# The first expert stage loads whole 2 MiB weight units into five homes, in place of 1 MiB halves into eleven

## The reference

```
logits = (xt @ w_router) + b_router
top_v, top_i = lax.top_k(logits, TOP_K);  gates = softmax(top_v)
y = sum over e of dense_gate[:, e] * ((silu(xt @ w1[e]) * (xt @ w3[e])) @ w2[e])
```

## Time and profile before

| what | value |
|---|---|
| median of 3 runs | 1507.8 us (1507.69 to 1508.5) |
| profiled execution | 1507.31 us |
| its span, first to last instruction | 1505.5 us |
| PE busy | 1423.2 us, 95% |
| DVE busy | 841.7 us, 56% |
| ACT busy | 566.9 us, 38% |
| bytes moved, mean rate | 443.45 MB, 295 GB/s |
| granted TensorE clock, mean | 0.99 |

### The profile page before, as it was taken

One profiled execution on the slowest core, in us unless ns is written; L12 is line 12 of the kernel. 1 busy time (PEld: TensorE's weight loads), 2 busy tenths in 40 slices (PEclk: granted clock), 3 DMA queues, 4 the chain that ended last, 5 costly groups with the idle time before them and its releaser, 6 DMA issues.

```text
span 1505.5 us, 24226 instructions
## 1 busy us (share of the span) xinstructions
PE 1423.2 (95%) x10246; PEld 1001.3 (67%) x10246; DVE 841.7 (56%) x1358; ACT 566.9 (38%) x838; POOL 32.7 (2%) x32
## 2 busy tenths in 40 slices
PE   6999999999999999999899988999999999999987
PEld 6988879999988888873588437984443443443435
DVE  5777697899979679940589107772211212112127
ACT  5673337464443447730477003432111111110115
POOL 0000101000030000000000001000000000000001
PEclk9999999999999999999999999999999999999999
DMA  9441026454441239999999994599999999999991
GB/s 355 163 168 59 2 95 228 176 213 179 168 155 60 84 126 418 408 365 409 406 419 370 420 420 167 203 427 378 426 427 425 427 427 427 427 426 427 425 420 56
DMA packets 48354, 443.45 MB, mean 295 GB/s; under 512 B 6768, under 2 KB 7280, under 8 KB 17008
## 3 DMA queue, kind: packets, MB, share of 16 engines
q1 hardware_dynamic: 47088, 438.36, 71.7%
q10 hardware_dynamic: 1152, 3.46, 0.6%
HBM read 440.75 MB, written 1.05 MB: 293 GB/s over the span
## 4 chain that ended last, share of the span: by engine, by line
PE 74%; DVE 12%; DMA 8%; ACT 3%; issue 2%; PEldq 0%; DVEq 0%; ACTq 0%; PEld 0%; SPq 0%
PE psum L239 72%; DMA sb_spare<-moe_up 3%; DMA sb_work<-moe_up 3%; DVE sb_ring_r L1280 2%; DMA sb_ring<-moe_last 1%; DMA sb_work<-moe_last 1%; DVE sb_work L3040 1%; PE psum L2825 1%; DVE sb_ring_r L298 0%; PE psum L2230 0%; DVE sb_work L1374 0%; DVE sb_ring_r L524 0%; DVE sb_ring_r L2152 0%; DVE sb_work L1800 0%; DVE sb_work L1372 0%
## 5 line engine op out<-in xcount | busy, mean ns | idle before, releaser
L239 PE MATMUL psum<-sb_work 128*64 128x512 f32 (+13 forms) x3548 | 323.6, 342 | 23.5 <-DVE sb_work L3040 7.8
L239 PEld LDWEIGHTS psum<-sb_work 128*64 128x64 f32 (+5 forms) x3548 | 161.7, 143 | 160.7 <-issue 139.1
L239 PE MATMUL psum<-sb_ring,sb_work 128*64 128x512 f32 (+2 forms) x660 | 159.0, 599 | 12.7 <-DMA sb_ring<-moe_last 5.2
L239 PE MATMUL psum<-sb_xT_r,sb_ring_r 128*128 128x256 f32 x512 | 143.9, 283 | 0.0
L239 PE MATMUL psum<-sb_split 128*128 128x512 f32 (+1 forms) x398 | 128.7, 382 | 0.0
L239 PEld LDWEIGHTS psum<-sb_ring,sb_work 128*64 128x64 f32 (+1 forms) x660 | 51.5, 141 | 104.2 <-issue 98.1
L3038 DVE TENSOR_TENSOR sb_work<-sb_work,psum 128x512 f32<-128x512 f32 x16 | 11.0, 688 | 167.9 <-ACT sb_work L2950 167.9
L2950 ACT ACTIVATE sb_work<-psum 128x512 f32<-128x512 f32 x16 | 9.6, 598 | 240.2 <-PE psum L239 240.2
L239 PEld LDWEIGHTS psum<-sb_xT_r,sb_ring_r 128*128 128x128 f32 x512 | 98.2, 192 | 0.3
L3008 DVE SCALAR_TENSOR_TENSOR sb_out_even<-psum,sb_work,sb_out_even 128x512 fp32r<-128x512 f32 x32 | 22.6, 747 | 125.8 <-ACT sb_out_even L2936 125.8
L239 PE MATMUL psum<-sb_split,sb_lnp_r 128*128 128x512 f32 (+1 forms) x260 | 87.7, 376 | 4.1 <-DVE sb_ring_r L2152 3.7
(11 more groups left out here) (514 smaller groups left out, 2876.6 us busy)
## 6 DMA issues: line engine op xcount, KB each, us to landing
sb_work<-moe_up SPq DMA_DIRECT2D x33, 2048.0 KB, 25.8
sb_ring<-moe_wide SPq DMA_DIRECT2D x52, 1024.0 KB, 9.6
sb_ring<-w_dense SPq DMA_DIRECT2D x23, 2048.0 KB, 8.7
sb_work<-moe_wide SPq DMA_DIRECT2D x43, 1024.0 KB, 10.6
sb_ring<-moe_up SPq DMA_DIRECT2D x18, 2048.0 KB, 25.3
sb_work<-moe_down SPq DMA_DIRECT2D x17, 2048.0 KB, 24.0
sb_ring<-ffn_wide SPq DMA_DIRECT2D x14, 2048.0 KB, 7.5
sb_ring<-moe_down SPq DMA_DIRECT2D x9, 2048.0 KB, 25.2
```

The source lines that it names most:

```text
L239: return nc.tensor.matmul(o, lhsT, rhs, start=start, stop=stop, **kw)
```

## The change

Loads are made per unit and no longer per half. `M1_LOADS` has one entry per unit and expert (72 in place of 144); there are five homes of 4096 columns: the three ring slots and two in `work`. The eleventh home is given up. A home may be refilled when half b of the unit in it was used. The first unit comes in three pieces (a quarter, a quarter and a half of it), so its half a is waited for on a semaphore of its own. The readers still go by halves, but both halves of a unit land together.

```diff
-        M1_HOMES = (2, 3, 4, 5, 0, 1, 6, 7, 8, 9, 10)
-        LAST_DOWN = 2 * M1_STREAM.index("d2")
+        M1_HOMES = (1, 2, 0, 3, 4)
         M1_LOADS = []
         for m in range(len(MEMBERS)):
-            own_loads = [(m, i, j) for i in range(NH) for j in range(len(MEMBERS[m])) if not (m > 0 and packed(m - 1) and i < 2)]
+            own_loads = [(m, s, j) for s in range(len(M1_STREAM)) for j in range(len(MEMBERS[m]))
+                         if not (m > 0 and packed(m - 1) and s == 0)]
             if packed(m) and m < LAST_MEMBER:
-                own_loads[-PACK * (NH - LAST_DOWN):-PACK * (NH - LAST_DOWN)] = [(m + 1, 0, 0), (m + 1, 1, 0)]
+                own_loads[-PACK:-PACK] = [(m + 1, 0, 0)]
             M1_LOADS += own_loads
...
         def half_raw(m, i, j=0):
-            return home_columns(ring, work[:, SPLIT_AT + HOMES_AT:], emb.rearrange("p h d -> p (h d)"), M1_LOAD_AT[m, i, j], half_size(i))
+            return home_columns(ring, work[:, SPLIT_AT + HOMES_AT:], M1_LOAD_AT[m, i // 2, j], half_first(i), half_size(i))
...
         def half_loaded(eng, m, i, j=0):
-            n = M1_LOAD_AT[m, i, j]
-            eng.wait_ge(home_sem(n), 16 * (n // len(M1_HOMES) + 1) + (32 if n % len(M1_HOMES) == HOMES2 else 0))
+            if (m, i) == (0, 0):
+                eng.wait_ge(sem("first_loaded"), 48)
+                return
+            n = M1_LOAD_AT[m, i // 2, j]
+            eng.wait_ge(home_sem(n), 16 * (n // len(M1_HOMES) + 1))
...
         def m1_load_used(eng, n):
-            m, i, _ = M1_LOADS[n]
-            eng.wait_ge(sem("m1_pe"), M1_PE[m, M1_HALVES[i]])
+            m, s, _ = M1_LOADS[n]
+            eng.wait_ge(sem("m1_pe"), M1_PE[m, M1_STREAM[s] + "b"])
...
-                    to = half_raw(m, i, j)
+                    to, first = unit_raw(n), 0
                     if n == 0:
                         sp.dma_start(to[:, 0:QUARTER], src[:, 0:QUARTER]).then_inc(sem("piece_loaded0"), 16)
-                        to, words = to[:, QUARTER:], slice(QUARTER, HALF)
-                    sp.dma_start(to, src[:, words]).then_inc(home_sem(n), 16)
+                        sp.dma_start(to[:, QUARTER:HALF], src[:, QUARTER:HALF]).then_inc(sem("first_loaded"), 16)
+                        first = HALF
+                    sp.dma_start(to[:, first:], src[:, first:unit_size(unit)]).then_inc(home_sem(n), 16)
```

More of the change, by code:

```diff
@@ L2078, in m1_home, with home_columns, unit_size, unit_raw @@
             return M1_HOMES[(n + HOME_SHIFT) % len(M1_HOMES)]
-        def home_columns(ring_tile, rest, last, n, size):
+        def home_columns(ring_tile, rest, n, first, size):
             h = m1_home(n)
[L2083 to L2087, removed]
+            if h < RING:
+                return ring_tile[:, h, first:first + size]
+            at = UNIT * (h - RING) + first
             return rest[:, at:at + size]
+        def unit_size(s):
+            return half_size(2 * s) + half_size(2 * s + 1)
+        def unit_raw(n):
+            return home_columns(ring, work[:, SPLIT_AT + HOMES_AT:], n, 0, unit_size(M1_LOADS[n][1]))
         def half_raw(m, i, j=0):
-            return home_columns(ring, work[:, SPLIT_AT + HOMES_AT:], emb.rearrange("p h d -> p (h d)"), M1_LOAD_AT[m, i, j], half_size(i))
+            return home_columns(ring, work[:, SPLIT_AT + HOMES_AT:], M1_LOAD_AT[m, i // 2, j], half_first(i), half_size(i))
         def half_low(m, i):
-            return home_columns(ring_r, split[:, HOMES_AT:], m1_emb, M1_LOAD_AT[m, i, 0], half_size(i))
+            return home_columns(ring_r, split[:, HOMES_AT:], M1_LOAD_AT[m, i // 2, 0], half_first(i), half_size(i))
         def home_sem(n):
-            r = n % len(M1_HOMES)
-            return sem("first_loaded" if r == HOMES2 else f"home_loaded{r}")
+            return sem(f"home_loaded{n % len(M1_HOMES)}")
         def half_loaded(eng, m, i, j=0):
-            n = M1_LOAD_AT[m, i, j]
-            eng.wait_ge(home_sem(n), 16 * (n // len(M1_HOMES) + 1) + (32 if n % len(M1_HOMES) == HOMES2 else 0))
+            if (m, i) == (0, 0):
[3 more added lines that the diff above has]
+            eng.wait_ge(home_sem(n), 16 * (n // len(M1_HOMES) + 1))
         def half_number(m, i):
@@ L2116, in m1_load_used @@
         def m1_load_used(eng, n):
-            m, i, _ = M1_LOADS[n]
-            eng.wait_ge(sem("m1_pe"), M1_PE[m, M1_HALVES[i]])
+            m, s, _ = M1_LOADS[n]
+            eng.wait_ge(sem("m1_pe"), M1_PE[m, M1_STREAM[s] + "b"])
         def m1_home_loads(r):
-            return len(range(r, len(M1_LOADS), len(M1_HOMES)))
+            return len(range(r, len(M1_LOADS), len(M1_HOMES))) if r < len(M1_HOMES) else 0
         def m1_last_loads(s):
-            return [n for n in range(len(M1_LOADS) - len(M1_HOMES), len(M1_LOADS)) if m1_home(n) // 2 == s]
+            return [n for n in range(len(M1_LOADS) - len(M1_HOMES), len(M1_LOADS)) if m1_home(n) == s]
         def split_high(act, m, i):
@@ L3691, in _ @@
                 expert_at = {}
-                for n, (m, i, j) in enumerate(M1_LOADS):
+                for n, (m, unit, j) in enumerate(M1_LOADS):
                     position = MEMBERS[m][j]
@@ L3697, in _ @@
                         m1_load_used(sp, n - len(M1_HOMES))
-                    s, words = M1_STREAM[i // 2], slice(half_first(i), half_first(i) + half_size(i))
+                    s = M1_STREAM[unit]
                     src = I["moe1_wide"][expert_at[position], WIDE.index(s)] if s in WIDE else I["moe1_last"][expert_at[position], NARROW.index(s)]
-                    to = half_raw(m, i, j)
+                    to, first = unit_raw(n), 0
                     if n == 0:
                         sp.dma_start(to[:, 0:QUARTER], src[:, 0:QUARTER]).then_inc(sem("piece_loaded0"), 16)
-                        to, words = to[:, QUARTER:], slice(QUARTER, HALF)
-                    sp.dma_start(to, src[:, words]).then_inc(home_sem(n), 16)
+                        sp.dma_start(to[:, QUARTER:HALF], src[:, QUARTER:HALF]).then_inc(sem("first_loaded"), 16)
+                        first = HALF
+                    sp.dma_start(to[:, first:], src[:, first:unit_size(unit)]).then_inc(home_sem(n), 16)
                 overflow_sync(sp, 0)
```

## The result

The changed kernel takes 1522.0 us (median of 4 runs, 1519.3 to 1528.4) against 1508.0; the ratio is 1.0098, 95% interval 1.0074 to 1.0121, that is **+14.8 us** (+11 to +18); the two medians differ by 14.0. Forecast were 1512.8 us, +5.0. The direction was right, the size a third of it, and 1522.0 lies outside the forecast range of 1507.0 to 1517.5. The profiled execution took 1519.3 us (span 1517.5), the fastest of the four. Its first expert load is issued at 549.75 us and not at 551.28, so times of the stage are compared as distances from this issue.

The account below looks back on a forecast made before the run. It took the expert stage to end with the DMA stream, set back by homes freed late: member 3 begins 3.0 us later, d2 of member 5 5.0 later in all, so 1507.8 + 5.0 = 1512.8 us, range 1507.0 to 1517.5.

Parts of the forecast that it names:

- The mechanism of member 2: Member 2: u1' must wait for all of u0, not only u0a; 3.4 us of depth lost, landing 7.5 us after issue.
- The start: First expert loads: u0a lands only with u0b, delaying the first splits; cost 0.3 us, bounds 0 and 2.5.
- u1 of member 3: Member 3's tight load: ready at 759.5, PE comes at 760.7; covered by about 1 us, else PE loses 0 to 1.
- Behind u1' the queue stays fed: pairs are released 2 or more loads ahead: Member 2: the 5 wide and 6 narrow units left take 46.6 us, so d2' lands at 735.6, d2 4.0 us later.
- u1' waits for u0 ... landing at 863.7: Member 5: u0 used at 856.2, u1' lands 7.5 us later; 41.7 us of loads follow, the last landing at 905.4.
- the queue's bound: Member 2: queued behind g1' and u1, u1' would land at 687.9; issue at 681.5 plus 7.5 decides, 1.1 us later.
- The clock: Packed members: low level after PE's waits; member 2 called even, member 3 begins +2.0 or +4.0 (taken +3.0), member 5's d2 +4.3 to +6.2.
- Rate beats depth: Rival: lost depth is hidden in the expert stage and faster transfers take all 6.2 us off, 1501.6 us; chance 0.10.
- No change: Rival: PE's waits spread out, never reaching the low clock, lone loads near the queue's bound; +1.1, 1508.9 us; chance 0.22.
- The much slower rival: Rival: the start loses 2.5 us, u1 of member 3 1 us, low clock in both packed members 2.2; +10.7, 1518.5; chance 0.08.
- signs named for being right: Deeper rate dips, lone units 7 to 9 us, PE's waits from d0, d2 near 735.6 (member 2) and 906 (member 5).
- signs named for being wrong: Member 2's d2 at or before 731.6, PE waiting on splits in members 0, 1, 3, 4, or granted clock at 1.00 throughout.

Follow-up runs that it names:

- experiment 5: The change with dummy matmuls on PE ahead of its waits for loads in members 2 and 5, half as many as in an earlier try: +11.5 us, ratio 1.0076.
- late rows: The change with ACT's load of the norm's rows (1 MiB) issued only after the last expert load landed, not at the start of member 5: +11.2 us, ratio 1.0074.
- experiment 3: The change with each unit loaded in two transfers of a half, readers waiting for both halves, homes freed by unit: +15.8 us, ratio 1.0105.

## Why the prediction was wrong

**What held.** The bytes and the place did: all is lost in the packed members, behind u0. The mechanism of member 2 came out to the tenth. u1' was issued when u0 was used and took 7.5 us; the loads issued then, and the one that waited for member 3's g0, in the kernel after:

```profile
679.62 0.85 SPq L3710 DMA_DIRECT2D sb_work<-moe_wide  x2
...
749.94 0.33 SPq L3710 DMA_DIRECT2D sb_ring<-moe_wide  x1
```

and the time to landing of u1' of member 2 (issued at 679.62) and of member 5 (858.55):

```profile
sb_work<-moe_wide SPq DMA_DIRECT2D x1, 2048.0 KB, 7.5
```

```profile
sb_work<-moe_wide SPq DMA_DIRECT2D x1, 2048.0 KB, 10.2
```

A full queue's units landed 4.90 us apart and narrow ones 3.70 (4.91 and 3.68 were taken). The start cost nothing in place of 0.3: members 0 and 1 are done at 111.8 in both. Members 3 and 4 took 96.3 us in both, so u1 of member 3 was covered.

**The step that failed** is the sentence "Behind u1' the queue stays fed: pairs are released 2 or more loads ahead", and with it the 46.6 us of the loads behind u1'. From the landing of u1' (687.2) to that of d2' (736.9, PE starts at 737.04) it took 49.8 us, 3.2 more. The loss has two parts, of about the same size.

The first comes directly behind u1', before PE has waited for more than 0.41 us. d0 was issued 0.5 us behind u1', but landed 6.46 us after it and not 4.91:

```profile
sb_work<-moe_wide SPq DMA_DIRECT2D x1, 2048.0 KB, 13.5
```

So a queue that had almost run dry (u1, the last load in it, landed 1.4 us after u1' was issued) delayed two loads: the first landed 7.5 us after its issue, as I had priced it, the second 13.5 us after its own, where 7.5 + 4.91 - 0.5 = 11.9 had been priced. d0' made up 0.15 us of it, so that 1.4 us of the 3.2 are lost here.

The second part is the one I had left out of the working: I had worked out when PE would wait, for d2, but not carried a wait back into the releases that follow it. PE waits 4.12 us for d0' and gets the low clock; d0 is used at 707.3, and only then are the loads of u2' and d1 issued (707.47 and 707.98), when the queue has one load left, to land at 709.5. u2', d1 and d1' then land 4.34, 6.07 and 4.75 us apart, 1.7 us more than a full queue's. The rate falls with PE at work all the time, in this window after:

```profile
707.00:714.00 7.00, 7.00 (x60) 4.04 (x58) 0.00 (x0) 0.92 (x3) 0.00 (x0) 1.00 0.82 312
```

From the issue of u1' to the landing of d2' the forecast had 7.5 + 46.6 = 54.1 us; it took 57.3, and 56.1 with dummies in place of the waits (experiment 5). So the clock behind the waits makes 1.2 us of the 3.2.

**Member 5** had the same mistake at another place. "u1' waits for u0 ... landing at 863.7" took 7.5 us for a lone load, and I didn't ask for the queue's bound. It took 10.2, because the queue was behind already: g1, three loads ahead of it, landed at 853.40, and three loads at 4.90 us make 868.1, where u1' landed at 868.7. The bound as I had worked it out in member 2, from an idle queue at the issue of g1' (847.7 + 7.5 + 2 x 4.9 = 865.0), would have missed it too. That is 2.7 us; from there to the last landing it was 41.8 us against 41.7. Whether the norm's 1 MiB was part of it is open: late rows left it at 9.5.

**The clock** was mis-sized. I called member 2 even and took the middle; the low level came in d0 and in d2 of member 2 and in d1 of member 5, where PE began d2 2.6 us behind the last landing (913.11, 910.5) in place of 1.0.

**The sum by terms**, as distances from the first issue. d2 of member 2 begins 7.0 us later (forecast 4.0): 3.2 more by the queue, 0.3 less by the start, 0.1 of rest. Member 3 begins 6.8 later (forecast 3.0): those 3.0 again and 0.8 of the clock, since d2 took 7.07 us, near the 7.2 of before, where the forecast had the middle between that and 5.2. In member 5 the forecast added 2.2 and the trace 6.6: 2.7 by u1', 1.6 because PE began d2 2.6 us behind the last landing and not 1.0 (d1 had waited 4.42 us and run at the low level), 0.1 of rest. That makes 13.4 in the traces; the 14.8 of all runs has 1.4 more, which one pair of traces doesn't show. The forecast's own middle is a little off: that of 3.3 to 7.2 is 5.2 or 5.3, and I wrote 5.0.

**The rivals.** "Rate beats depth" is refuted by its own sign: d2 of member 2 begins 7.0 us later and not sooner. With equal homes and equal waits, 71 more transfers cost 1.0 us (experiment 3), and 6.2 lies just outside what the two intervals leave room for. The full queue is faster by 0.09 us per unit (2.097 MB at 419 and at 427 GB/s), but where the queue is full the time isn't set. "No change" (1508.9) is out by the interval. The much slower rival (1518.5) was the nearest in size, by the wrong reason: neither the start nor u1 of member 3 took part. What neither it nor my forecast had is the size of depth: the forecast priced 3.4 us of later issue for 1 MiB less and unit grain together, and the runs give 5.9 and 7.7 us for each alone.

**The signs.** Of the signs named for being right, the dips are deeper (by 8 and 20 GB/s over 32 us), a lone unit took 7.5 us, though the other 10.2, and PE's waits begin ahead of d0, even with 0.41 us at u1. The two starting times of d2 came out too late: 7.0 us later in member 2, where 4.0 was forecast, and 13.4 in member 5, where 5.2 was. None of the signs named for being wrong appeared.

## What to carry to other kernels

Where a queue of prefetches feeds an engine that alternates between being slower and faster than the loads, count the depth in bytes that can be in flight while a home is still held, not in homes: a home twice as large, held until all of it was used, is a loss of depth even where the total is equal. Work the releases out to the end of the stretch, with each wait of the consumer entered into the releases behind it, since a wait late in the loop starves the queue once more. Price a dry queue by more than its first load: the second one was late as well. Before giving a cost to the clock, make the same edit in both kernels: here dummy matmuls helped both, and the difference stayed at 14 us. And test whether transfers are limited one by one before merging them: queued 1 MiB loads were within 2% of 2 MiB ones.

## What the runs showed of the hardware

A 2 MiB load issued while the one before it is still landing can land later than both bounds, a lone load's 7.5 us and 4.9 us behind its forerunner. With late rows, one issued at 848.15, its forerunner landing at 851.0, landed at 857.7, 1.8 us past the later bound. And landings can be far apart with all DMA engines at work: from 687.2 to 693.6 the next load, d0 of member 2, took 6.46 us while they were busy and moved 428 GB/s, in this window after:

```profile
687.00:693.70 6.70, 6.40 (x30) 2.65 (x32) 0.00 (x0) 1.01 (x2) 0.00 (x0) 1.00 1.01 428
```

The DMA packets in the trace show where the bytes went. When u1 landed, 681.0, nothing behind it in the queue had been moved yet. When u1' landed, 0.17 MB of the loads behind it had been moved, and when d0 landed, 0.80 MB of those behind it: 0.64 MB more, or 1.5 us at 428 GB/s, which is what d0 was late by. So no time of the engines was lost there; a part of it went to loads whose turn came later. In experiment 5 the same shows one load sooner: 0.62 MB ahead when u1' landed (8.6 us after its issue), 0.66 at d0 (4.88 us later). Which of the 16 engines came last isn't in the record, so why they run ahead of one another stays open.
